# Split operands for all tiles of an input projection, and three reordered chains in the block behind it

## The reference

```
for l in range(2):
    proj = (rms(x) * g1) @ w_in[l]                  # 1024 x 7680: q k v | r k v lora | retention | gates
    mixed = g0 * (attention @ w_attn_o) + g1 * (rwkv7 @ w_rwkv_o) + g2 * (retention @ w_ret_o)
    x = x + mixed @ w_out[l]
    x = x + (silu(h2 @ w_gate[l]) * (h2 @ w_up[l])) @ w_down[l]
x = x + mLSTM and Hyena mixer(x)                    # log-sigmoid gate rows, running sums and maxima
x = x + experts(x)                                  # 16 experts, each takes the 32 tokens with the
x = rms(x) * g_final                                # highest probability in its row of the router
```

## Time and profile before

| | us |
|---|---|
| runs | 2408.12, 2407.77, 2402.48; median 2407.77 |
| the profiled execution, and its span | 2401.93, 2400.1 |
| PE busy, of the span | 1961.1 (82%) |
| DVE busy | 854.9 (36%) |
| ACT busy | 451.6 (19%) |
| POOL busy | 29.9 (1%) |

### The profile page before, as it was taken

One profiled execution on the slowest core, in us unless ns is written; L12 is line 12 of the kernel. 1 busy time (PEld: TensorE's weight loads), 2 busy tenths in 40 slices (PEclk: granted clock), 3 DMA queues, 4 the chain that ended last, 5 costly groups with the idle time before them and its releaser, 6 DMA issues.

```text
span 2400.1 us, 29326 instructions
## 1 busy us (share of the span) xinstructions
PE 1961.1 (82%) x12744; PEld 1391.7 (58%) x12744; DVE 854.9 (36%) x1188; ACT 451.6 (19%) x447; POOL 29.9 (1%) x21
## 2 busy tenths in 40 slices
PE   7999999999999999999989878556655655655655
PEld 6987789999998789999658663111111111111111
DVE  6645458556655447654346640000000000000002
ACT  3523013333432112332231111000000000000000
POOL 0000000000000010000000000000000000000000
PEclk9999999999999999999989979888788788788787
DMA  6443635656443534556423238999999999999996
GB/s 236 169 140 106 237 106 159 202 156 194 162 145 134 196 147 141 174 156 194 155 70 141 105 141 350 417 417 417 418 417 418 417 417 417 417 417 417 417 417 262
DMA packets 232068, 613.17 MB, mean 255 GB/s; under 512 B 11229, under 2 KB 106845, under 8 KB 198365
## 3 DMA queue, kind: packets, MB, share of 16 engines
q1 hardware_dynamic: 229744, 602.19, 66.2%
q10 hardware_dynamic: 2220, 9.45, 1.1%
HBM read 610.55 MB, written 1.05 MB: 255 GB/s over the span
## 4 chain that ended last, share of the span: by engine, by line
PE 55%; SPq 30%; DMA 6%; DVE 5%; issue 2%; ACT 2%; ACTq 0%; DVEq 0%; PEldq 0%
SPq L1365 30%; PE PS L1471 10%; PE PS L1527 8%; PE PS L1520 8%; PE PS L1522 7%; PE PS L620 5%; DMA work<-in_w_gate 2%; DMA work<-in_w_up 1%; DMA ring<-in_w_gate 1%; PE PS L826 1%; PE PS L1453 1%; DMA ring<-in_w_down 1%; PE PS L761 1%; PE PS L1694 1%; PE PS L1571 1%
## 5 line engine op out<-in xcount | busy, mean ns | idle before, releaser
L826 PE MATMUL PS<-work,proj 128*32 128x512 f32 x1024 | 155.5, 742 | 102.4 <-DMA work<-in_w_up 66.5
L1471 PE MATMUL PS<-hT,ring 128*128 128x256 f32 x896 | 200.3, 383 | 0.0
L826 PE MATMUL PS<-ring,proj 128*32 128x512 f32 x768 | 124.4, 780 | 90.7 <-DMA ring<-in_w_up 51.2
L1309 DVE TENSOR_TENSOR proj<-proj,PS 128x512 f32<-128x512 f32 x16 | 11.0, 688 | 503.1 <-PE PS L826 503.1
L1471 PEld LDWEIGHTS PS<-hT,ring 128*128 128x128 f32 x896 | 169.5, 191 | 24.8 <-issue 1.7
L2139 DVE TENSOR_TENSOR ring_low<-ring,high_f 128x4096 fp32r<-128x4096 f32 (+1 forms) x38 | 146.8, 3864 | 58.1 <-ACT high_f L1955 58.1
L1955 ACT ACTIVATE high_f<-ring 128x4096 fp32r<-128x4096 f32 (+1 forms) x38 | 120.8, 3178 | 220.4 <-PE PS L1527 186.9
L826 PEld LDWEIGHTS PS<-work,proj 128*32 128x32 f32 x1024 | 31.3, 123 | 218.2 <-DMA work<-in_w_up 107.0
L1520 PE MATMUL PS<-xh_f,high_f 128*128 128x256 f32 x640 | 153.6, 280 | 0.3
L1522 PE MATMUL PS<-hT_low,high_f 128*128 128x256 f32 x624 | 151.1, 283 | 0.0
L620 PE MATMUL PS<-hT,ring 128*128 128x256 f32 (+1 forms) x576 | 131.1, 387 | 4.4 <-ACT hT L952 4.4
(11 more groups left out here) (458 smaller groups left out, 3229.0 us busy)
## 6 DMA issues: line engine op xcount, KB each, us to landing
ring<-in_w_in SPq DMA_DIRECT2D x74, 1024.0 KB, 7.4
work<-in_w_gate SPq DMA_DIRECT2D x64, 1024.0 KB, 20.9
work<-in_w_up SPq DMA_DIRECT2D x64, 1024.0 KB, 26.6
work<-in_w_down SPq DMA_DIRECT2D x64, 1024.0 KB, 23.6
ring<-in_w_gate SPq DMA_DIRECT2D x48, 1024.0 KB, 22.4
ring<-in_w_up SPq DMA_DIRECT2D x48, 1024.0 KB, 26.9
ring<-in_w_down SPq DMA_DIRECT2D x48, 1024.0 KB, 18.4
ring<-in_w_ada SPq DMA_DIRECT2D x24, 1024.0 KB, 7.3
```

Source lines behind the costliest of these rows:

```text
L826: mm = nt.matmul(PS[32 * j:32 * j + 32, 2 + n // 4, :], x(k), w[:, F_E * kk + 512 * j:F_E * kk + 512 * (j + 1)], start=(k == 0), stop=(k = ...
L1471: mm = nt.matmul(PS[:, bank(l, q), T * b:T * (b + 1)], weight(b, k), moving(k), start=(k == 0), stop=(k == kn - 1))
```

## The change

1. Tiles 16 to 29 become split too (`tile_highs` on ACT, `tile_lows` on DVE, `tile_part` and `tiles` on PE). ACT and DVE work by tile, not by slot: two pieces of 128x1024 each, read from the ring as 8 x 128 columns of every 512. The high parts lie in the blocks of `proj` that later gates fill, and from tile 23 on in four free places. The low part of the activations now overwrites hT.
2. PE can run half a tile (`tile_part(q, b)`). Beside the softmax of rounds 1 and 2 stand three halves, beside the copies one half. The cuts of `solve` move, and `solved_blocks` moves behind the third round. `diagonal_blocks` is cut in two. The memset of GM waits for tile 29 in its last third, because XH_A lies there.
3. mLSTM: the gate rows come before the convolution on DVE, their exp and ln before the filter spectra on ACT; LF and BB move to a place of their own.
4. Router: logits by k first; ACT loads the exp table early and takes the exp before the token copies; PE zeroes two output banks while DVE looks for the best; the last replace is dropped, the indices are spread before they are copied.
5. Last expert: both half slots before the scatter; ACT takes the squares; the output leaves in three pieces.

```diff
@@
-BESIDE_SOFTMAX = [(22, 24), (25, 26), (27, 28)]
-BESIDE_COPY = [(24, 25), (26, 27), (28, 29)]
-SOLVED = [8, 10, 20, 22, BLOCK - 1]
+BESIDE_SOFTMAX = [[(22, 0), (22, 1), (23, 0), (23, 1)], [(24, 1), (25, 0), (25, 1)], [(26, 1), (27, 0), (27, 1)]]
+BESIDE_COPY = [[(24, 0)], [(26, 0)], [(28, 0)]]
+SOLVED = [10, 10, 14, 16, 22, 24, BLOCK - 1]
@@ PE, second block
             def route():
-                for t in range(TT):
-                    for k in range(KD):
...
+                for k in range(KD):
+                    pe.wait_ge(h2_ready, KD + k + 1)
+                    for t in range(TT):
...
                 pe.wait_ge(topk_done, 1)
+                pe.wait_ge(dve2, 4)
+                zero_banks(YB[2:4])
+                pe.wait_ge(diag_ready, 1)
+                nt.matmul(PS[:, 3, :], ones[0:EXPERTS, :], DIAG[0:EXPERTS, :], start=True, stop=True).then_inc(row_ready, 1)
+                pe.wait_ge(topk_done, 2)
@@ PE, last_expert
                 down_half(pair, EXPERT_SLOTS + 10, 0)
+                down_half(pair, EXPERT_SLOTS + 11, 1)
                 pe.wait_ge(ye_ready, 2 * e + 1)
                 scatter(0, 2)
                 scatter(2, 4)
-                down_half(pair, EXPERT_SLOTS + 11, 1)
-                norm_sums(3, 0, 4)
-                pe.wait_ge(ye_ready, 2 * e + 2)
+                pe.wait_ge(ye_last, 1)
@@ PE, layers
+            def tile_part(l, q, b):
+                n = q // 2
+                out, w = PS[:, bank(l, q), T * b:T * (b + 1)], ring_low[:, n % RING, :]
+                h, first = tile_high(q, b), tile_columns(q, b)
+                if b == 0:
+                    pe.wait_ge(high_ready, part_count(l, n, q % 2))
+                    taken(l, q)
+                for k in range(KD):
+                    nt.matmul(out, h[:, P * k:P * (k + 1)], XH_A[:, k, :], start=(k == 0), stop=False)
+                    nt.matmul(out, h[:, P * k:P * (k + 1)], hT_low[:, k, :], start=False, stop=False)
+                if b == 0:
+                    pe.wait_ge(low_dve, part_count(l, n, q % 2))
+                for k in range(KD):
+                    c = 512 * k + first
+                    mm = nt.matmul(out, w[:, c:c + P], XH_A[:, k, :], start=False, stop=(k == KD - 1))
+                if b == 1:
+                    mm.then_inc(block_done, 1)
@@ ACT, layers
+            def tile_highs(l, *qs):
+                for q in qs:
+                    n = q // 2
+                    act.wait_ge(ring_full[n % RING], full(l, n))
+                    act.wait_ge(block_done, done(l, max(q - 2, 15) if q > 16 else 13))
+                    if q == 23:
+                        act.wait_ge(bonus_ss, 1)
+                    if q == 24:
+                        act.wait_ge(bonus_out, 1)
+                    for b in range(2):
+                        c = tile_columns(q, b)
+                        w = ring[:, n % RING, :].rearrange("p (k c) -> p k c", c=512)[:, :, c:c + P]
+                        ins = na.activation(tile_high(q, b).rearrange("p (k c) -> p k c", c=P), w, ACT.Copy)
+                    ins.then_inc(high_ready, 1)
@@ ACT, attention
-                proj_out(l, 20, 22)
+                proj_out(l, 20, 21)
+                tile_highs(l, 22, 23)
+                proj_out(l, 21, 22)
                 act.wait_ge(att_tr, 2)
                 na.activation(KDUP[:, :, :].rearrange("p a b -> p (a b)"), PS[:, 5, :], ACT.Copy).then_inc(att_kv, 1)
+                tile_highs(l, 24)
@@ DVE, attention, in each round
+                    if rnd == 0:
+                        tile_lows(l, 23)
+                    solve(SOLVED[2 * rnd], SOLVED[2 * rnd + 1])
...
+                    tile_lows(l, 24 + 2 * rnd)
+                    solve(SOLVED[2 * rnd + 1], SOLVED[2 * rnd + 2])
+                    tile_lows(l, 25 + 2 * rnd)
+                solved_blocks()
@@ DVE, mlstm
                 dve.wait_ge(act2, 6)
+                nv.scalar_tensor_tensor(lf, f, -1.0, f, ALU.mult, ALU.max).then_inc(gate_rows, 1)
                 conv(QK2, 0, P2_CQW, P2_CQB, 0, 8, 8)
-                dve.wait_ge(kf_ready, 8)
-                nv.scalar_tensor_tensor(lf, f, -1.0, f, ALU.mult, ALU.max).then_inc(gate_rows, 1)
```

More of the change, by code:

```diff
@@ L109, with part_count @@
 SPLIT_A = 8
-SPLIT = list(range(SPLIT_A)) + list(range(S_OUT, LAYER_SLOTS))
+TILED = list(range(SPLIT_A, N_PROJ // 2))
+SPLIT = list(range(SPLIT_A)) + TILED + list(range(S_OUT, LAYER_SLOTS))
+PARTS = len(SPLIT) + len(TILED)
+def part_count(l, n, half=1):
+    before = sum(2 if m in TILED else 1 for m in SPLIT if m < n)
+    return PARTS * l + before + (half + 1 if n in TILED else 1)
 C_ID, C_ONES, C_BD, C_PERM, C_DUP, C_COS, C_SIN = 0, 128, 256, 384, 512, 768, 1024
@@ L572, in second_sync @@
             y = io["yT"].rearrange("(k p) t -> p k t", p=P)
-            for half in range(2):
-                k = slice(4 * half, 4 * half + 4)
-                sp.wait_ge(h2_ready, 2 * KD + 1 + half)
+            for n, last in enumerate(OUT_ENDS):
+                k = slice(OUT_ENDS[n - 1] + 1 if n else 0, last + 1)
+                sp.wait_ge(h2_ready, 2 * KD + 1 + n)
                 sp.dma_start(y[:, k, :], hT[:, k, :]).then_inc(out_done, 16)
-            sp.wait_ge(out_done, 32)
+            sp.wait_ge(out_done, 16 * len(OUT_ENDS))
         def second_pool(pool):
@@ L895, in first_expert @@
                     hidden(first, 0, n)
-                pe.wait_ge(dve2, 4)
-                for b in YB:
-                    mm = nt.matmul(PS[:, b, :], ZERO, con[:, 0:512], start=True, stop=False, skip_group_check=True)
-                mm.then_inc(scattered, 1)
+                zero_banks(YB[0:2]).then_inc(scattered, 1)
                 rest(0, 0, 0)
@@ L1059, in second_scalar @@
             act.wait_ge(expert_slots, EXPERT_SLOTS * (EXPERTS + 1))
-            na.activation(YE2, PS[:, 4, :], ACT.Copy).then_inc(ye_ready, 1)
+            na.activation(YE2, PS[:, 4, :], ACT.Copy).then_inc(ye_last, 1)
+            na.activation(bias[:, 3:4], onec, ACT.Sqrt)
+            for n in range(4):
+                x = slice(2 * n, 2 * n + 2)
+                act.wait_ge(moe_sum, n + 1)
+                na.activation(SQ2[:, x, :], xT[:, x, :], ACT.Square).then_inc(sq2, 1)
             root(3)
@@ L1533, in split_product, with tiles, tile_parts @@
                 mm.then_inc(block_done, 1)
+            def tile_part(l, q, b):
[15 more added lines that the diff above has]
+                    mm.then_inc(block_done, 1)
+            def tiles(l, *qs):
+                for q in qs:
+                    tile_part(l, q, 0)
+                    tile_part(l, q, 1)
+            def tile_parts(l, parts):
+                for q, b in parts:
+                    tile_part(l, q, b)
             def norm_sums(m, lo, hi):
@@ L1542, in norm_sums @@
                     mm.then_inc(ss_ready, 1)
-            def project(l, lo, hi):
-                for q in range(lo, hi):
-                    s, half = q // 2 % RING, q % 2
-                    if half == 0:
-                        pe.wait_ge(ring_full[s], full(l, q // 2))
-                    product(l, q, lambda b, k: ring[:, s, 512 * k + P * (2 * half + b):512 * k + P * (2 * half + b + 1)],
-                            lambda k: hT[:, k, :], KD)
             def split_project(l, lo, hi):
@@ L2372, in attention @@
                 rwkv_triangles(1)
[L2373 removed]
+                tile_lows(l, 20)
+                diagonal_blocks(0, 2)
                 dve.wait_ge(att_std, 1)
```

195 lines of the change are left out of this document (118 added, 77 removed).

## The result

The changed kernel takes 2368.15 us (median of four runs, 2362.94 to 2369.91), the kernel before 2406.1 us in the same session (2402.48 to 2408.12): ratio 0.984, 95% interval 0.982 to 0.9861. The forecast was 2380 us with a range of 2366 to 2393. The profiled execution took 2362.94 us, the lowest of the four, with a span of 2360.9 us against 2400.1. So the two traces differ by 39.2 us, the medians by 38. The sum had 23.5.

What follows compares the result with a forecast made beforehand. PE's work bounds the attention layers, DMA the experts. Terms 14 (layers) + 4.2 (mLSTM) + 4.5 (router) + 0.8 (end) = 23.5 us off the profiled 2401.9 give 2378.4; forecast 2380 us, range 2366 to 2393.

Steps and rivals of the forecast that it cites:

- Part 1, tiles: Attention layers: split tiles cut PE's work 17.6 us per layer, about 10 stay; 20.6 us for both before the clock.
- the walk: PE, ACT and DVE lists followed instruction by instruction from 111 us: idle 12.3 us, tile 29 of layer 0 ends at 235.3.
- The clock's term: Attention layers: two clock falls per layer at 1.7 us, 3.4 per layer, reducing 20.6 to 14 us.
- Part 2, mLSTM: mLSTM gate rows: ready when PE ends its tile, PE goes on at 1246.2 instead of 1250.45, 4.2 us.
- Part 3, router: Router logits to first gather: gather starts 3.1 us earlier, 1.4 more from the clock; 4.5 us, bounds 3.0 and 5.5.
- Part 4, end: Last expert: scatters and sums in one piece after the last half slot; 0.8 us, bounds -1.5 and 1.5.
- The clock holds through the gaps: Rival, layers: no falls, 30 us gained, 2374, or 2370 with the mLSTM gap as well; chance 0.14.
- Somewhat slower: Rival: ACT and DVE take 3.0 and 3.3 us per tile, layers give nothing, 2394; chance 0.1.
- Pieces at half rate: Rival: strided pieces take ACT and DVE 3.6 and 4.4 us per tile, 2418; chance 0.04.
- The gain does not arrive: Rival: second block's gain is lost because the experts' weights are late for another reason, 2386; chance 0.05.
- The tiles were never the time: Rival, layers: an unseen wait (PSUM bank of q - 2) holds PE; no chance of its own given.
- The anchor: Forecast 2380 set between 2378.4, from the profiled execution's 2401.9, and the median 5.8 us above that execution.

Runs made afterwards that it cites:

- e2: Kernel before with only the second block's new order (gates, router, last expert), old tiles: 2391.73 us, ratio 0.9946.
- e9: The changed kernel repeated unaltered, for a second profile and a comparison on one chip: 2368.58 us, ratio 0.9855.
- e12: Changed kernel with ACT making each high part of tiles 16 to 29 twice: 2396.89 us, ratio 0.9973.
- e1: Kernel before with only the fourteen new tiles, second block as it was: 2381.26 us, ratio 0.9915.
- e10: Repeat of e5's kernel, on one chip with the changed kernel's repeat: 2350.09 us, ratio 0.9777.
- e3: Changed kernel with ACT's high part of tile 24 behind the exponential of round 0 instead of ahead: 2359.91 us, ratio 0.9825.
- e4: Changed kernel with tile 21's low part ahead of the last two diagonal transposes, k's copy ahead of tile 23's high part: 2355.75 us, ratio 0.9811.
- e5: Changed kernel with high part of 24, low part of 21 and copy of k reordered, solve's steps handed out anew: 2350.13 us, ratio 0.9779.
- e6: Changed kernel with the old order of the mLSTM gates on ACT and DVE, Silu at its old place: 2374.39 us, ratio 0.988.

## Why the prediction was right, and where not

- **Part 1, tiles: the walk held.** Tile 29 of layer 0 was forecast for 235.3 us and ends at 235.36. ACT's two pieces take 2.00 us (2.05 taken), DVE's 2.35 (2.33). Part of the agreement is luck: the waits were 1.66, 2.25 and 1.89 us where I had 1.9, 2.75 and 2.4, and 2.8 in rounds 1 and 2 where I had 5.2, 8.6 in all instead of 12.3; in return PE began 0.4 late, one fall of the clock cost 1.7, which the walk did not have, and PE's own work shrank by 16.3 instead of 17.6 (behind another kind of matmul the first ones are 0.2 us apart instead of 0.12, and a half tile that stands alone took 3.0 to 3.3 us instead of 2.87). Without its fall tile 29 would have ended near 233.7, so the walk was about 2 us per layer too slow, counted with the late start.
- **The clock's term was the step that failed.** I took 6.8 us off the layers for two falls per layer, on top of the walk, and kept 14. The layers gave 22.9 between the first two traces. First, the changed kernel's had one fall per layer there; counted in stretches of 3.4 us at 0.50, both layers together have 2, and in the five other profiles of the same layers 2, 4, 4, 4 and 6. Second, I charged falls to the change alone: the old tiles fall too, once in the kernel before and three times in e2. The 1.7 us of layer 1, which I had read in the earlier trace rows and used as the price, belong to both kernels: the fall behind the two-column matmuls is absent in the changed kernel's first profile and back in e9's. The term should have been a difference of two uncertain counts: 1.7 us between the first two traces (one stretch against two), 2 to 3 over all profiles (two against 3.7 on average), where I had 6.6 to 6.8. Without the clock the layers would have given 24.6, where the walk had 20.6. So of the 8.9 us that I was short, 4.9 are the clock's term and 4.0 the walk's waits. Over all profiles the second block begins at 1156.0 us with the old layers (two) and 1133.2 with the new (six): 22.8.
- **Part 2, mLSTM**: 4.2 forecast, 4.9 to 5.9 measured. The transposes follow PE's tile at once, and 2.61 us of idle time are left for load and exponential: of the waits 4.25 us went, as forecast. A little of the "up to 4.4 more" arrived: the tile behind took 8.27 us instead of 8.87.
- **Not in the sum**: the unedited stretch, 3.3 us in nine profiles of ten with the new gates.
- **Part 3, router**: 4.5 forecast, 4.8 between the traces, but otherwise made up. The gather starts 15.3 us behind the logits (19.1 before), 3.8 where I had 3.1; another 1.6 came from the logits, 5.39 us instead of 7.01, by the clock; and the gather, which I had running at the upper level, took 6.2 us instead of 5.6, since the clock came up only at 1408.8.
- **Part 4, end**: 0.8 forecast, and none of it is there where the clock cost neither order anything (14.13 and 14.18). The 3.8 us of the traces were the clock's.
- **Rivals.** "The clock holds through the gaps" named 2374 and 2370, both nearer to the median of 2368 than my 2380. Its reason failed: the clock fell behind the gaps in every profile of these rounds. Its number came near because the falls of the old layers offset part of the new ones and the walk was too slow. "Somewhat slower" did not occur (2.00 and 2.35 us per tile, not 3.0 and 3.3). "Pieces at half rate" did not occur either, and e12 shows that its half on ACT would have cost what the walk says. "The gain does not arrive" is refuted: from the first expert to the last half slots the kernel takes 927.5 us before and 927.9 after, at a DMA share of 1.02 from 1412 to 2320 us. "The tiles were never the time" is refuted by e1.
- **The anchor.** The forecast added 1.6 us for a profiled run below the median. The changed kernel's median is 5.2 us above its own profiled run. By medians the gain is 36 to 38 us; of the 12 to 14 missing about 9 are the layers' (5 the clock's term, 4 the walk's waits), 3 the unedited stretch, 1 to 2 the mLSTM. That the median still lies inside the range is owed to its lower bound, which took every term at its best.

## What to carry to other kernels

When a change moves work from the bound engine to two idle ones, walk the three lists instruction by instruction: a busy share under half does not tell whether a step is late, and the walk gave both the size of the result and, later, the three misplaced steps and the new cuts of the solve that brought another 18 us. Where the clock falls now and then, charge it on both sides or on neither, and take one trace for one draw: the same kernel's stages differ from profile to profile by 3 to 5 us. Of two traces, compare stages that nobody edited first; what they differ by is what the edited ones may owe to chance.

## What the runs showed of the hardware

- **The clock falls with PE busy.** In e10 PE was busy for 7.00 of 7.00 us before the clock fell near 697 us, right behind the 20 two-column matmuls, as in layer 1 of the kernel before. The same fall stands in layer 1 of e3, e4 and e9 (702 to 704 us) and in both layers of e2 (160 and 723 us), but not in the changed kernel's first profile or e5's, which run the same matmuls. The Trainium skill (TensorE: Matmul & The Clock Gate, What's actually happening) ties a fall to idleness of the engine. These rows disagree with it; the rounds of e5 and e10, where no wait is above 1.3 us and no fall is left, agree.
- **Falls follow gaps, but not each gap.** In both layers of the seven profiles with the changed rounds' first waits (1.66 and 2.25 us within 9 us; in layer 1 of e3 and e9 only the second) a fall came, in 13 of 14 cases within 2.3 us of the second one's end; in layer 0 of e6 it came near 187 us, behind the wait of 1.89 us. That third wait was followed by a fall in 4 of 12 cases, and waits of 0.7 to 1.4 us in none. The waits of 3.7 to 4.3 us in e12 brought 17 us at 0.50 per layer. Why the same code falls at one place in one execution and not in the next stays open.
- **A strided piece costs little more than a plain one.** Two pieces of 8 runs of 128 columns, 1024 columns each, take ACT 2.00 us and DVE 2.35. Half of a plain slot of 4096 columns takes 1.82 and 2.22.
